# A decoder trunk layer on one core: both blocks of 128 tokens together, or one whole pass after the other with the weights streamed twice

## The reference

```python
proj = h @ w_in            # hq, hf, hi, hg, aq (2048 each), ckv (256), aiq (2048), aik (128), aiw (16), gate_a, gate_b (2048 each)
ya = hgrn2_branch(hq, hf, hi, hg, ...) @ w_branch_a      # gated recurrence over time, chunks of 64, 16 heads of 128
yb = dsa_branch(aq, ckv, aiq, aik, aiw, ...) @ w_branch_b # each token attends to its 64 best causal keys, 16 heads
mix = (sigmoid(gate_a) * ya + sigmoid(gate_b) * yb) @ w_mix_out
h = layer_norm(ALPHA * h + mix)
h = layer_norm(ALPHA * h + memory_cross_attention(h, mem, w_q, w_k, w_v, w_o))   # 4 heads of 512
# PEER: q = h @ w_query; per head (8) the 16 best of 128 x 128 experts by two half keys
h_e = gelu(h . expert_u[e]);  y = sum over the token's 128 experts of gate * h_e * expert_v[e]
h = layer_norm(ALPHA * h + y)
```

## Time and profile before

| | |
|---|---|
| median of the runs shown | 3219.8 us |
| span of the profiled execution | 3215.5 us |
| its time beside the span | the median lies 4.3 us above the span |
| TensorE busy | 2962.7 us (92%) |
| weight loads (PEld) | 2146.8 us (67%) |
| DVE busy | 1016.7 us (32%) |
| ScalarE busy | 593.4 us (18%) |
| POOL busy | 740.1 us (23%) |
| moved by DMA | 838.92 MB, 261 GB/s over the span |

### The profile page before, as it was taken

The page is one execution under the profiler, slowest core; times in us unless marked ns, Lnnn a source line. Parts: engine busy times, 40 slices in busy tenths (PEclk is TensorE's granted clock), DMA queues, the critical chain, the costliest instruction groups (busy, mean ns, idle before and its releaser), DMA issues. The chain is left out here.

```text
span 3215.5 us, 31981 instructions
## 1 busy us (share of the span) xinstructions
PE 2962.7 (92%) x11512; PEld 2146.8 (67%) x11512; DVE 1016.7 (32%) x1670; ACT 593.4 (18%) x1305; POOL 740.1 (23%) x551
## 2 busy tenths in 40 slices
PE   8999999999999999999999999987788878888887
PEld 7888888888888888888888875543333333333332
DVE  0121121002000111112000188887444454444444
ACT  1221221100001222001101032232111122222222
POOL 0000000000000000000000044545555555555553
PEclk9999999999999999999999999999888888888888
DMA  6733333443443333454433669999999999999997
GB/s 266 205 130 130 135 149 134 170 157 131 157 157 138 144 127 128 160 206 183 151 130 126 235 248 406 375 371 422 422 422 422 422 422 422 422 422 422 422 422 323
DMA packets 99097, 838.92 MB, mean 261 GB/s; under 512 B 11041, under 2 KB 11089, under 8 KB 15825
## 3 DMA queue, kind: packets, MB, share of 16 engines
q0 software_dynamic: 78000, 560.33, 42.8%
q1 hardware_dynamic: 21024, 277.56, 23.2%
HBM read 832.60 MB, written 5.24 MB: 261 GB/s over the span
## 5 line engine op out<-in xcount | busy, mean ns | idle before, releaser
L479 PE MATMUL PS<-arena 128*128 128x256 f32 x8256 | 1796.3, 379 | 9.2 <-DMA arena<-units 8.4
L479 PEld LDWEIGHTS PS<-arena 128*128 128x128 f32 x8256 | 1560.7, 190 | 222.9 <-issue 12.6
L806 PE MATMUL PS<-arena 128*128 128x512 f32 x2048 | 999.8, 651 | 212.4 <-DMA arena<-peer_v,arena 198.6
L806 PEld LDWEIGHTS PS<-arena 128*128 128x128 f32 x2048 | 423.4, 210 | 785.0 <-issue 538.1
L1590 DVE CUSTOM_DVE_ANT_0 arena<-arena 128x2048 f32<-128x2048 f32 x256 | 586.8, 2292 | 141.5 <-DMA arena<-peer_u,arena 132.6
L435 POOL DMA_INDIRECT arena<-peer_v,arena x256 | 392.5, 1533 | 504.9 <-PE PS L806 465.3
L411 POOL DMA_INDIRECT arena<-peer_u,arena x256 | 320.0, 1250 | 216.5 <-DVE arena L1582 133.5
L371 POOL DMA_DIRECT2D arena<-w_ukv x8 | 4.3, 534 | 600.0 <-PE PS L627 600.0
L1190 ACT ACT_TABLE_LOAD x46 | 59.0, 1283 | 377.2 <-DVE arena L1590 355.5
L1582 DVE COPY arena<-arena 128x4 uint32 (+1 forms) x64 | 11.6, 181 | 366.7 <-DMA arena<-peer_v,arena 260.7
L1190 ACT ACTIVATE arena<-arena 128x1 f32<-128x1 f32 x256 | 51.9, 203 | 397.4 <-DVE arena L1590 324.3
(11 more groups left out here) (229 smaller groups left out, 1115.1 us busy)
## 6 DMA issues: line engine op xcount, KB each, us to landing
arena<-units SPq DMA_DIRECT2D x129, 2048.0 KB, 7.7
arena<-ln_rows POOLq DMA_DIRECT2D x5, 1024.0 KB, 8.7
arena<-mem_cols POOLq DMA_DIRECT2D x2, 2048.0 KB, 29.3
arena<-w_ukv POOLq DMA_DIRECT2D x8, 512.0 KB, 3.6
arena<-peer_u,arena POOLq DMA_INDIRECT x256, 11.4
arena<-peer_v,arena POOLq DMA_INDIRECT x256, 11.7
rb_scratch<-arena POOLq DMA_DIRECT2D x1, 3072.0 KB, 37.6
arena<-x_cols SPq DMA_DIRECT2D x4, 512.0 KB, 8.4
```

Of the source, the lines that this page charges most:

```text
L479: ins = mm(bank[:, n * 256:n * 256 + rhs.shape[1]], lhs, rhs, start=k == 0, stop=k == KT - 1)
L806: ins = mm(Y[c], diag[:, e * P:(e + 1) * P], v_rows[e][:, c * 512:(c + 1) * 512], start=False, stop=True, skip_group_check=True)
```

## The change

The whole trunk runs for tokens 0-127 (pass 0) and then for tokens 128-255 (pass 1), as straight code without loops. Of the 130 units, pass 1 leaves out CK and CV: their results for all of mem are made in pass 0, stored to HBM and read back by heads in pass 1. The other 114 units are loaded a second time. The ring has three buffers instead of four. The recurrence goes by four heads of 128 tokens (`QUADS`), its state after pass 0 is kept in `states`. Units are taken in pairs, so that a PSUM bank holds 512 columns again.

```diff
+def units_of(tb):
+    return [u for u in range(UNITS) if tb == 0 or not (U_CK <= u < U_IQ or U_CV <= u < U_CQ)]
+PLACE = {(tb, u): tb * UNITS + n for tb in range(TB) for n, u in enumerate(units_of(tb))}
...
+            def unit(tb, u, step, at, rows, act_t, width=P, halves=(0, 1), ks=range(KT), inputs=None, cols=UN):
...
+                parts = 2 if not rows or width > P else 1
...
                     for k in ks if n == halves[0] else range(KT):
...
                         if rows:
+                            lhs = act_t[:, k * width + n * P:k * width + (n + 1) * P]
                             rhs = w[:, k * UN:k * UN + cols]
...
                         else:
+                            lhs = w[:, k * UN + n * P:k * UN + (n + 1) * P]
+                            rhs = act_t[:, k * width:(k + 1) * width]
...
+            def pair(tb, u, step, rows, act_t, inputs=None):
+                unit(tb, u, step, 0, rows, act_t, inputs=inputs)
+                unit(tb, u + 1, step, UN, rows, act_t)
```

`width` is 128 but for CK and CV (256). Some loads that were POOL's are now SP's, between the units, each with its wait:

```diff
+            def load_unit(tb, u):
+                p = PLACE[tb, u]
+                if p >= RING:
+                    sp.wait_ge(proj_done, p - RING + 1)
+                sp.dma_start(W[p % RING], units[stored_at(u)]).then_inc(w_landed[p % RING], 16)
+
+            def load_bias(tb, g):
+                n, g_all = group(tb), groups_before(tb) + g
+                if g >= 2:
+                    sp.wait_ge(bias_rd, g_all - 1)
+                else:
+                    sp.wait_ge(sel_done, tb + 1)
...
+                    if u == U_AQ + 2:
+                        for g in range(2):
+                            load_bias(tb, g)
```

The experts of block 0 are taken during pass 1. A row has one of three buffers (five from the 17th expert of block 1 on, when two of the ring's buffers are used). Products stay on DVE; the sums for block 0 are now DVE's too, over `acc` of 2048 columns, and ScalarE takes gelu for four experts at once. Both engines have "turns" at the same places of the pass:

```diff
+            for s in range(SLOTS):
+                gather_u(s)
+            for s in range(TB * NE):
+                gather_v(s)
+                if s + SLOTS < TB * NE:
+                    gather_u(s + SLOTS)
...
+            def sum_batch(n):
+
+                dve.wait_ge(gelu_done, n + 1)
+                gh = gh4[n % 2]
+                link(v.tensor_tensor(gh, gates[0][:, n * BATCH:(n + 1) * BATCH], hg4[n % 2], ALU.mult))
+                for e in range(BATCH):
+                    s = BATCH * n + e
+                    b, nth, _ = ROWS[s]
+                    dve.wait_ge(v_in[b], 16 * (nth + 1))
+                    mark(v.scalar_tensor_tensor(acc, v_rows[b], gh[:, e:e + 1], acc, ALU.mult, ALU.add), v_summed, s + 1)
...
+            def turn():
+
+                n, second = divmod(turns[0], 2)
+                if second:
+                    sum_batch(n)
+                else:
+                    dot_batch(n)
+                turns[0] += 1
```

`gather_u(s)` waits for the product, `gather_v(s)` for the sum that used the buffer before. There are 64 turns: on DVE four in each of the four bodies of the recurrence, three behind it, nine at the index scores and WA, eight in attention, four at WB, four at MIX and the first norm, four at the heads of cross-attention, three at CO (51 in all up to the second norm), and 13 behind it:

```diff
+            trunk(0)
+            link(v.tensor_scalar(acc, H0, ALPHA, None, ALU.mult))
+            for k in range(1, 4):
+                choose(0, k)
+            weigh(0, 0)
+            trunk(1)
+            turn()
+            for k in range(1, PEER_HEADS):
+                if turns[0] < 2 * BATCHES:
+                    turn()
+                choose(1, k)
+                if k == 1:
+                    weigh(1, 0)
+            while turns[0] < 2 * BATCHES:
+                turn()
+            weigh(1, 1)
...
+            for e in range(PK):
+                dot(NE + e)
+            last_norm(0, [acc[:, c * 512:(c + 1) * 512] for c in range(4)], acc)
+            for e in range(PK, NE):
+                dot(NE + e)
+            dve.wait_ge(v_used, NE)
+            last_norm(1, B, fin_x)
```

More of the change, by code:

```diff
@@ L150, in inside @@
             return region[:, at:at + n]
[L153 to L156, removed]
+        w_ring = take(RING * 4096)
+        W = [inside(w_ring, 4096 * s, 4096) for s in range(RING)]
+        rows_area = take(2 * SLOTS * D)
         C = take(K_END)
+        R_X, R_O, R_M, R_B, H0, H1, acc = (take(D) for _ in range(7))
+        S = take(8192)
+        scores = take(D)
@@ L194, in trunk_layer @@
[L194 to L223, removed]
@@ L235, in trunk_layer @@
-        fin_g = inside(R_K, D, D)
-        fin_b = [inside(C, K_MEAN, 512), inside(C, K_MEAN + 512, 512), inside(R_S, 12288, 512), inside(R_S, 12800, 512)]
-        fin_x = inside(w_ring, 2 * D, D)
+        gates = [take(NE) for _ in range(TB)]
+        experts = [take(NE).bitcast(U32) for _ in range(TB)]
+        v16 = take(32)
+        i16 = take(32).bitcast(U32)
+        i16f = take(32)
+        top_s = take(PK)
+        pos = take(PK).bitcast(U32)
+        posh = take(2 * PK).bitcast(U32)
+        poshf = take(2 * PK)
@@ new lines, in sparse_body @@
+            def sparse_body(tb, j):
+                actions = (keys_values, logits, turn_probs, attend)
+                for n in range(8):
+                    name, u = ("AQ", U_AQ + 4 * j + n // 2) if n < 4 else ("GB", U_AQ + 4 * j + n // 2)
+                    unit(tb, u, (tb, name, j), n // 2 % 2 * UN, False, xt, halves=(n % 2,))
+                    if j and tb == 0 and n % 2:
+                        actions[n // 2](0, j - 1)
+                    elif j and tb == 1:
+                        actions[n % 4](1, 2 * (j - 1) + n // 4)
@@ L866, in _, with queries @@
[L866 to L878 removed]
+            def queries(tb, k, inputs=None):
+                unit(tb, U_PQ + k, (tb, "PQ", k), 0, False, h_t, inputs=inputs)
@@ new lines, in exps @@
+            def exps(tb, g):
+                n, g_all = group(tb), groups_before(tb) + g
+                width = 512 // n
+                act.wait_ge(lg_rd, g_all + 1)
+                for h in range(n):
+                    cols = lg[:, h * width:(h + 1) * width]
+                    ins = fn(cols, cols, ACT.Exp, bias=nmax[:, h:h + 1], accum_out=esum[:, h:h + 1])
+                    if h == n - 1:
+                        mark(ins, p_exp, g_all + 1)
+                    else:
+                        chain.link(ins)
```

2236 lines of the change are left out of this document (1148 added, 1088 removed).

## The result

Four executions of the changed kernel took 3352.52 to 3363.7 us, median 3354.1; four of the kernel before, on the same chip, 3218.2 to 3220.2, median 3219.1. The ratio is 1.0424 (95% interval 1.041 to 1.0439). The direction was right and the time lies inside the range, but the forecast of 3282 us gave the change 62 us and it cost 135. The profiled execution was the slowest of the four: 3363.7 us with a span of 3361.4.

A forecast was written before the change was run, and what follows sets the result against it. The prediction took the trunk before as TensorE-bound and the experts as DMA-bound, and pass 1 as DMA-bound after: 1160 + 1240 + 231 + 635 + 12 = 3278, given as 3282 us, 1.9% slower, range 3190 to 3410.

The forecast's parts named there:

- Pass 0: Trunk for tokens 0-127, to its last PQ unit: 1160 us, from weight units, other matmuls and uncovered steps.
- rival 4: Loads of stationary tiles bind the matmuls, a unit costing 12.2 us: 3780 us in all, chance 0.02.
- The terms of pass 1: Tokens 128-255 beside block 0's experts: TensorE 912, DVE some 910, DMA 1151 us; DMA binds, with losses 1240.
- TensorE's sum: TensorE in pass 1: 80 x 7.25 + 26 x 6.91 = 760, + 92, + bare chains 60: 912 us.
- the price of the weights: DMA in pass 1: 106 weight units at 5.7 us each, from 369 GB/s, 604 us.
- The length of a turn: DVE's group of four expert products or sums: 10.4 to 15.5 us, taken as 12, with 51 in pass 1.
- Losses of DMA time: Pass 1: DMA idle 55 us where nobody consumes and 35 us while only the ring asks, 90 us together.
- The tail: After the trunk: 13 turns and eight choices left on DVE, which binds, 231 us; 56 us of DMA lost.
- Block 1's experts: After the tail, 128 experts at 4.97 us each, with small corrections: 635 us.
- Rival 2: The chains bind: pass 1 follows DVE with turns at 15.5 us, pass 1380 us, 3460 in all, chance 0.09.
- Rival 1: Near-perfect overlap of queues, gathers filling DVE's own time: 3157 us; with half the losses 3205 to 3220; chance 0.18.
- Rival 3: TensorE's granted clock falls in pass 1; at 0.65 it needs 1370 us and binds: 3410 us, chance 0.05.

The follow-up runs named there:

- without turns: Changed kernel with all 64 turns (groups of four expert products or sums on DVE) moved behind the trunk, so pass 1 runs alone: 3682.9 us.
- turns of two: Changed kernel with DVE turns of two products and two sums instead of four of one kind, gathers queued in that order: 3219.3 us, ratio 1.0004 to the kernel before.
- short units: Changed kernel with each pass 1 weight unit except the queries of PEER loading 512 of its 4096 columns: 3145.1 us.
- all edits: Changed kernel with two-product, two-sum turns, block 1's later choices among its products, and its u rows asked three ahead of v rows: 3144.9 us, ratio 0.9774 to kernel before.
- short products: Changed kernel with two-product, two-sum turns and block 0's products and sums over 128 of 2048 columns: 3137.8 us.

## Why the prediction was right in direction and wrong in size

**Pass 0: right.** A query unit of 64 records, in order of time:

```profile
1118.04 7.31 PE L569 MATMUL PS<-arena 128*128 128x128 f32 x64
```

7.31 us against 7.41 in the earlier trace rows; rival 4, stationary loads that bind, is dead. The first choice came at 1104 against 1110, and the pass ended at about 1154 against 1160.

**The terms of pass 1: right but for two.** 457 MB against 451; without turns the pass took 904 us against the 912 of TensorE's sum (beside the turns its matmuls took 919 instead of the 852 in that sum, at a lower clock); a sum row 2352 ns, the 2.35 us taken between 2.29 and 3.0; DVE's work, turns included, 642 us against 51 x 9.4 + 110 + 40 = 630. Of the two, one is the turn, below. The other is the price of the weights, at which the forecast took the 369 GB/s of the earlier trace rows: 604 us and 39 for the rest of that queue. The queue's 241.5 MB filled 0.459 x 1281 = 588 us, that is 411 GB/s. So with turns of two the pass takes 1142 us, less than the 1151 of the transfers' sum.

**The length of a turn: the step that failed.** The forecast knew that a fourth row is asked for inside the turn and bounded the turn at 10.4 to 15.5 us, then took 12, "near the short end, since three of four rows were fetched during DVE's other work". Product turns measured 16.6 and sum turns 19.4, above the upper end. Two things were wrong. The landing came from the earlier trace rows, from a stretch in which only two query units were loaded beside the gathers; beside a ring that refills with 2 MB at a time it was 14 in the median and up to 40. And "near the short end" had no ground: that three of four rows are there doesn't shorten a turn whose fourth is asked for inside it. The fourth rows of pass 1 landed 11.5 us after their issue in product turns and 14.2 in sum turns, in the mean; the forecast's own 2.3 + 0.2 + landing + 2.3 gives 16.3 and 19.0, and 16.6 and 19.4 were measured. The formula was right, its landing was not. Third rows came late too in 11 sum turns, in part by the order of POOL's queue, and took 67 of the 437 us. In the forecast DVE's 910 us were 630 of work, 51 x 2.6 = 132 of waits for rows and 150 of other waits; measured are 642, 437 and a rest of 202, together 1281. The middle term is 305 us too small. With 437 in its place the DVE sum is 1215 us: above the 1151 of the transfers, though not yet above the 1240 that the forecast had with its losses; the rest, 202 instead of 150, does the remainder, and the limit changes hands. The short units cut the middle term by 247 us and the pass by 219, turns of two cut it by 220 and the pass by 140, down to what DMA allows.

**Losses of DMA time.** 90 us forecast, 164 measured, by the same cause; with turns of two 0.04 x 1199 = 48 us remain. The forecast listed places where nobody consumes and left out the turns themselves. (By its own figures, 5.7 of each 7.25 us over 200 us lose 43, not 35.)

**The tail.** DVE binds it, as forecast. But the sum of 231 us has a slip: it counts 13 turns and prices 12 (7 + 5), so by its own prices it is 243, and only 24 of the 36 us above forecast are left to explain. DVE's work is 201 us against 13 x 9.4 + 8 x 10.1 = 203. Its two forms that work on rows, 2435 to 2702 us:

```profile
L1397 DVE SCALAR_TENSOR_TENSOR arena<-arena 128x2048 f32<-128x2048 f32 x28 | 65.8, 2352 | 25.4 <-DMA arena<-peer_v,arena 24.7
L1381 DVE CUSTOM_DVE_ANT_0 arena<-arena 128x2048 f32<-128x2048 f32 x24 | 55.0, 2292 | 26.0 <-DMA arena<-peer_u,arena 25.4
```

50 us are waits for rows, where 12 x 2.6 = 31 were in the sum (34 with the thirteenth). Of the other 16 of the 66 us beside DVE's work, 8.5 are one wait, before the first choice, for ScalarE's evacuation of the query unit; the rest lies in gaps of under 1 us between instructions.

**Block 1's experts, 12 us more.** In three pieces:

```profile
2702.00:2742.00 40.00, 26.18 (x48) 10.30 (x48) 21.95 (x22) 8.48 (x25) 21.55 (x15) 0.81 0.88 362
...
2800.00:3300.00 500.00, 369.27 (x803) 144.78 (x802) 229.99 (x200) 89.89 (x300) 257.11 (x202) 1.00 1.01 421
3300.00:3349.00 49.00, 38.24 (x85) 15.11 (x83) 18.66 (x17) 8.67 (x26) 12.77 (x10) 1.00 0.83 343
```

The steady rate is the 421 to 422 GB/s of the earlier trace rows; 0.13 x 40 + 0.18 x 49 = 14 us are missing at the two ends, which the price of 4.97 us per expert had left out.

**The rivals.** Rival 2 (the chains bind, 3460 us) had the mechanism that decided, turns beyond 15 us, at a chance of 0.09. Its pass of 1380 us was 100 too long and isn't the sum of its named terms: 51 x 15.5 + 300 are 1090, and no row stood for the 290 of TensorE's waits on top; it also took a sum row of 3.0. Rival 1, near-perfect overlap, was wrong for this kernel, and its objection, slots and the chain from DVE, was the right one; but the objection was removable. With turns of two the stretch between the second norms is 1199 us, where the forecast comes to 1240 + 57 = 1297, and with all edits the kernel takes 3144.9, below this rival's 3157. Rival 3, the clock: 0.86 between the second norms against 0.98 with no turns, after waits for rows. For the same 7107 matmuls TensorE was busy 975.6 against 921.1 us, 54 more, beside 360 idle ones, so this rival's case, a TensorE that binds, did not come. The Trainium skill, "TensorE: Matmul & The Clock Gate" (why this matters for your kernels), says that the clock falls to half when matmuls have idle gaps; the trace goes with its direction, at a price of 54 us of busy time. How many of these lengthened the pass no run shows.

Pass 1 moved 357 GB/s. That is by chance the figure the Trainium skill, "SBUF — State Buffer" (summary of rules), counts HBM transfers at, about 358, but it is no ceiling here: the same stretch moved 395 with turns of two, 402 with short products too, and block 1 421. The mean of a stretch with a share of 0.87 is not a rate.

**How much of "slower" was luck.** The forecast had the kernel slower with DMA as the limit of pass 1. The kernel in which DMA nearly is the limit, with turns of two, took 3219.3 us, no slower than the kernel before. What made the changed kernel slower is the length of the turns, which the forecast had too short; its direction was right by a sum in which the transfers and their losses were priced too high and the turns too low.

**Open.** How much of the turns of two is due to the earlier asking and how much to the finer alternation of products and sums was not separated: turns of four with four slots for each table, or with u and v rows in an order that never holds one behind the other, were not tried.

## What to carry to other kernels

A consumer that works in groups larger than its buffers has the landing time of its last item inside each group (turns of two with three buffers took 140 us off this pass); make the group no larger than the number of buffers, look for requests that stand behind another table's in one queue, and price it with the landing measured beside the traffic that will be there, not beside less. Before an engine's idle share is taken as room, ask which of its steps stand in series with a transfer: here 642 us of work on DVE stretched over 1281. Work without a deadline (the choices) belongs into the stage that DMA binds, where 68 us of it cost about 5.

## What the runs showed of the hardware

- A gather of 1 MB (128 rows of 8 KB) landed after 13.9 to 14.3 us in the median beside 2 MB weight loads (40 at the most), after 8.4 beside loads of 0.26 MB, and after 7.9 with hardly any loads beside it. Weight units took 12.3 us to landing beside the gathers.
- Weight loads and gathers together moved 402 GB/s at a share of 0.98 over 1176 us, gathers alone 421 at 1.01: mixing them cost 5% at most here.
- An issue of a gather on POOL took 0.93 us at least and up to 2.93 us while a product or sum ran on DVE (true of 99 of the 101 issues over 1.1 us); the DMA share reached 0.96 with turns of two even so.
